# A delta-rule layer: the norms of queries and keys taken from transposed rows

## The reference, cut to what matters

```
def l2_norm(x):
    xf = x.astype(jnp.float32)
    return (xf * lax.rsqrt(jnp.sum(xf * xf, -1, keepdims=True) + EPS)).astype(x.dtype)

def deltanet_layer(x, valid, g_norm, w_in, conv_w, a_log, dt_bias, o_gain, w_out):
    ...
    z = h @ w_in
    qkv = jax.nn.silu(causal_dwconv(z[..., :2 * DN_KW + DN_VW], conv_w))
    ...
    q = l2_norm(q) * (DN_DK ** -0.5)
    k = l2_norm(k)
    ...
    o = gated_delta_rule(to_chunks(q), to_chunks(k), to_chunks(v), gate_chunks(g), gate_chunks(beta))
```

## Time and profile before

| what | value |
|---|---|
| median of 3 runs | 3075.04 us (3074.96 to 3075.6) |
| the profiled execution | 3068.84 us, of it the span 3066.8 us |
| TensorE busy | 2964.0 us, 97% of the span |
| VectorE busy | 1479.1 us, 48% |
| ScalarE busy | 798.5 us, 26% |
| GpSimd busy | 445.3 us, 15% |
| one-column products of the third layer | 160 records, 2191.8 to 2591.7 us |

### The profile page before, as it was taken

One profiled execution on the slowest core, in us unless ns is written; L12 is line 12 of the kernel. 1 busy time (PEld: TensorE's weight loads), 2 busy tenths in 40 slices (PEclk: granted clock), 3 DMA queues, 4 the chain that ended last, 5 costly groups with the idle time before them and its releaser, 6 DMA issues. The chain is left out here.

```text
span 3066.8 us, 38998 instructions
## 1 busy us (share of the span) xinstructions
PE 2964.0 (97%) x15091; PEld 1870.0 (61%) x15091; DVE 1479.1 (48%) x3453; ACT 798.5 (26%) x2045; POOL 445.3 (15%) x745
## 2 busy tenths in 40 slices
PE   5999999999999999799999999998999999999999
PEld 2445555555555554588787887654788888544444
DVE  2344544645545443555655665433445555443441
ACT  1113333323333321212323233221222222121230
POOL 0221221322212000121101112000001111111100
PEclk8999999999999999899999999999999999999999
DMA  7330001000113200421121211502421111030101
GB/s 248 130 145 28 28 28 54 30 28 28 35 49 90 76 1 21 148 62 53 45 76 46 66 49 51 176 1 83 110 56 29 29 41 44 1 114 26 55 1 55
DMA packets 137439, 186.78 MB, mean 61 GB/s; under 512 B 22284, under 2 KB 90540, under 8 KB 135204
## 3 DMA queue, kind: packets, MB, share of 16 engines
q1 hardware_dynamic: 136056, 184.21, 19.0%
q10 hardware_dynamic: 1200, 0.09, 0.0%
HBM read 174.61 MB, written 9.67 MB: 60 GB/s over the span
## 5 line engine op out<-in xcount | busy, mean ns | idle before, releaser
L488 PE MATMUL a_psP<-a_w,a_uT 128*128 128x512 f32 x1536 | 700.3, 601 | 7.5 <-DMA a_w<-a_w_in 7.5
L488 PEld LDWEIGHTS a_psP<-a_w,a_uT 128*128 128x128 f32 x1536 | 280.6, 192 | 325.0 <-issue 325.0
L737 DVE TENSOR_REDUCE a_small<-a_psS 128x1 f32<-128x768 f32 (+1 forms) x192 | 140.8, 775 | 402.0 <-PE a_psS L516 402.0
L1460 PE MATMUL b_psP<-b_w,b_uT 128*128 128x256 f32 x768 | 183.8, 382 | 1.0 <-DVE b_raw L1743 0.5
L643 ACT ACTIVATE a_e<-a_psS,a_small 128x768 f32<-128x768 f32 (+1 forms) x192 | 143.8, 753 | 139.1 <-DVE a_small L737 138.7
L1460 PEld LDWEIGHTS b_psP<-b_w,b_uT 128*128 128x128 f32 x768 | 141.7, 190 | 23.9 <-issue 3.9
L1780 DVE TENSOR_REDUCE b_small<-b_psS 128x2 f32<-128x512 f32 x64 | 44.3, 692 | 213.2 <-PE b_psS L1517 213.2
L650 ACT COPY a_pT<-a_psS 128x768 f32<-128x768 f32 (+1 forms) x96 | 63.0, 656 | 311.4 <-PE a_psS L525 311.4
L538 PEld LDWEIGHTS a_psO<-a_v,a_pT 128*128 128x128 f32 x896 | 115.1, 192 | 45.9 <-issue 45.9
L1617 ACT ACTIVATE b_e<-b_psS,b_small 128x512 f32<-128x512 f32 x128 | 86.7, 682 | 192.0 <-DVE b_small L1793 190.1
L1624 ACT COPY b_e<-b_psS 128x512 f32<-128x512 f32 x128 | 71.8, 587 | 228.6 <-PE b_psS L1527 147.4
(11 more groups left out here) (487 smaller groups left out, 5106.1 us busy)
## 6 DMA issues: line engine op xcount, KB each, us to landing
a_w<-a_w_in SPq DMA_DIRECT2D x16, 2048.0 KB, 9.0
b_w<-b_w_in SPq DMA_DIRECT2D x48, 512.0 KB, 3.8
a_yT<-mod_w SPq DMA_DIRECT2D x8, 1536.0 KB, 8.5
a_yT<-mod_w SPq DMA_DIRECT2D x8, 1024.0 KB, 17.5
b_yT<-b_w_in SPq DMA_DIRECT2D x16, 512.0 KB, 3.8
f_place<-bias_table SPq DMA_DIRECT2D x64, 128.0 KB
f_place<-a_w_in SPq DMA_DIRECT2D x16, 512.0 KB, 6.2
d_w<-a_w_in SPq DMA_DIRECT2D x16, 512.0 KB, 7.1
```

Source lines behind the costliest of these rows:

```text
L488: ins = nc.tensor.matmul(s.psP[:, x % 2, :], s.uT[:, a, t * P:(t + 1) * P], w[:, a, :], start=(a == 0), stop=(a == KD - 1))
L737: nc.vector.tensor_reduce(self.nm[i % 2][:, k:k + 1], self.score_banks(k, keys), AX_X, ALU.max, negate=True).then_inc(self.mx, 1)
L1460: ins = nc.tensor.matmul(out, lhsT, rhs, start=(a == 0), stop=(a == 3))
```

## The change

The squares are no longer summed by TensorE. Instead TensorE transposes the raw keys in step 0 (`key_rows`) and the raw queries in step 3 (`query_rows`) through `token_rows` into banks 5 and 6, so that tokens lie on partitions; ScalarE squares them out of these banks into `s.sq` (two ACTIVATEs each, 16 and 128 partitions); and VectorE adds up each token's 128 squares (`row_sums`: two reductions and the sum with epsilon). GpSimd's power is taken over five columns twice instead of ten once. The factors of the queries get a piece of their own in step 7 of VectorE's queue (`query_factors`).

The order changes with it. `log_decays` waits for ScalarE's squares of the keys. The pieces of `fold` in steps 3 and 4 (`BEHIND`) now come behind the projection products of their step, so `query_rows` stands behind the projections of step 3 and `query_products` behind those of step 4. On ScalarE the squares of the keys stand ahead of `tanh` in step 0, those of the queries at step 3 ahead of `copy_piece`, and the two squares of steps 9 and 10 are gone. On VectorE `query_sums` stands in step 5 ahead of two convolution passes.

```
@@ -1972,7 +1972,7 @@
         self.cv = sb("d_cv", [P, 2, TOK], F32)
-        self.sq = sb("d_sq", [P, 2, TOK], F32)
+        self.sq = sb("d_sq", [P, 2, CH * P], F32)
@@ -2233,7 +2233,7 @@
         chain.mark(nc.vector.tensor_scalar(row(EG), row(EG), 0.5, None, ALU.mult))
-        chain.mark(nc.vector.memset(s.ps[:, 6, 0:2 * CH], 0.0))
+        chain.mark(nc.vector.memset(s.tiny[:, 80:90], 0.0))
@@ -2264,6 +2264,7 @@
     PIECE = {1: 0, 3: 1, 4: 2, 5: 3, 7: 4, 9: 5, 10: 6, 11: 7}
+    BEHIND = (3, 4)
@@ -2274,11 +2275,13 @@
         (self.z, self.zc, self.cn, self.ct, self.si, self.gt, self.gz) = (sem("dh_" + n) for n in names)
-        names = ("squares", "square_sums", "sums_eps", "rstd", "factors", "log_decays", "decays", "kk",
+        names = ("key_squares", "key_rows", "sums_eps", "rstd", "factors", "log_decays", "decays", "kk",
                  "system", "kq", "attention", "keys_T", "keys_scaled", "values_T", "values_scaled", "first_level",
-                 "first_inverse_T", "first_inverse", "first_copied", "halves")
-        (self.sq, self.sm, self.se, self.rs, self.fa, self.gr, self.dm, self.kk, self.lt, self.kq, self.at,
-         self.tk, self.kd, self.tv, self.vb, self.b1, self.x1, self.x1T, self.x1c, self.hv) = (sem("df_" + n) for n in names)
+                 "first_inverse_T", "first_inverse", "first_copied", "halves", "query_rows", "query_squares",
+                 "query_sums_eps", "query_rstd", "query_factors", "row_sums")
+        (self.ks, self.kr, self.se, self.rs, self.fa, self.gr, self.dm, self.kk, self.lt, self.kq, self.at,
+         self.tk, self.kd, self.tv, self.vb, self.b1, self.x1, self.x1T, self.x1c, self.hv, self.qm, self.qs, self.qe,
+         self.qr, self.qf, self.rw) = (sem("df_" + n) for n in names)
@@ -2367,22 +2370,22 @@
-        def sums(h):
+        def key_rows(h):
                 self.prepare.gates_done(pe)
-            pe.wait_ge(self.sq, 2 * h + 2)
+            pe.wait_ge(self.si, 3 * h + 2)
                 pe.wait_ge(self.u0s, h - 1)
-            for r in range(2):
-                for t in range(CH):
-                    ins = nc.tensor.matmul(ps[0:chunk_len(t), 6, r * CH + t:r * CH + t + 1], s.sq[:, r, chunk_cols(t)],
-                                           s.masks[:, LEVELS + 1, 0:1], start=True, stop=True)
-            ins.then_inc(self.sm, 1)
+            token_rows(s.ck[:, h % 2, :], self.kr)
+
+        def query_rows(h):
+            pe.wait_ge(self.lt, h + 1)
+            token_rows(s.cq[:, h % 4, :], self.qm)
         def log_decays(h):
-            pe.wait_ge(self.se, h + 1)
+            pe.wait_ge(self.ks, h + 1)
@@ -2399,7 +2402,7 @@
         def query_products(h):
-            pe.wait_ge(self.lt, h + 1)
+            pe.wait_ge(self.qs, h + 1)
@@ -2432,7 +2435,7 @@
-        fold = {0: sums, 1: log_decays, 2: key_products, 4: query_products, 6: keys_T, 8: values_T, 10: first_inverse}
+        fold = {0: key_rows, 1: log_decays, 2: key_products, 3: query_rows, 4: query_products, 6: keys_T, 8: values_T, 10: first_inverse}
@@ -2581,7 +2584,7 @@
                             begin_rest(j)
-                if hf is not None and g in fold:
+                if hf is not None and g in fold and g not in self.BEHIND:
@@ -2589,6 +2592,8 @@
                         self.prepare.gate_sums(pe)
+                if hf is not None and g in self.BEHIND:
+                    fold[g](hf)
@@ -2622,12 +2627,12 @@
-        def squares(h, r):
-            act.wait_ge(self.si, 3 * h + r + 1)
+        def squares(h, r, rows, read, done):
+            act.wait_ge(rows, h + 1)
             if h:
-                act.wait_ge(self.sm, h)
-            x = s.cq[:, h % 4, :] if r == 0 else s.ck[:, h % 2, :]
-            nc.scalar.activation(s.sq[:, r, :], x, ACT.Square, scale=0.5).then_inc(self.sq, 1)
+                act.wait_ge(read, h)
+            nc.scalar.activation(s.sq[0:N_META, r, 0:P], ps[0:N_META, 6, P:2 * P], ACT.Square, scale=0.5)
+            nc.scalar.activation(s.sq[:, r, P:], ps[:, 5, :], ACT.Square, scale=0.5).then_inc(done, 1)
@@ -2689,7 +2694,10 @@
                     if g == 0:
+                        squares(hf, 1, self.kr, self.se, self.ks)
                         tanh(hf, 2)
+                    if g == 3:
+                        squares(hf, 0, self.qm, self.qe, self.qs)
@@ -2705,8 +2713,6 @@
                         tanh(hp, (6, 8).index(g))
-                    if g in (9, 10):
-                        squares(hp, g - 9)
@@ -2717,11 +2723,16 @@
         def rstd(h):
-            rs = s.tiny[:, 10:20]
             if h:
-                pool.wait_ge(self.fa, 5 * h)
-            nc.gpsimd.tensor_tensor(rs, s.tiny[:, 0:10], s.half[:, :], ALU.pow).then_inc(self.rs, 1)
+                pool.wait_ge(self.fa, 3 * h)
+            nc.gpsimd.tensor_tensor(s.tiny[:, 15:20], s.tiny[:, 5:10], s.half[:, 0:CH], ALU.pow).then_inc(self.rs, 1)
+
+        def query_rstd(h):
+            pool.wait_ge(self.qe, h + 1)
+            if h:
+                pool.wait_ge(self.qf, 2 * h)
+            nc.gpsimd.tensor_tensor(s.tiny[:, 10:15], s.tiny[:, 0:5], s.half[:, 0:CH], ALU.pow).then_inc(self.qr, 1)
@@ -2742,6 +2753,8 @@
                     rstd(hf)
+                if hf is not None and g == 5:
+                    query_rstd(hf)
@@ -2786,16 +2799,35 @@
+        def row_sums(h, r, chain):
+            raw = s.tiny[:, 80 + r * CH:80 + (r + 1) * CH]
+            nc.vector.reduce_sum(raw[0:N_META, 0:1], s.sq[0:N_META, r, 0:P], AX_X).then_inc(self.rw, 1)
+            nc.vector.reduce_sum(raw[:, 1:], by_chunk(s.sq[:, r, P:]), AX_X).then_inc(self.rw, 1)
+            dve.wait_ge(self.rw, 4 * h + 4 - 2 * r)
+            nc.vector.tensor_scalar(s.tiny[:, r * CH:(r + 1) * CH], raw, EPS, None, ALU.add).then_inc(chain, 1)
+
         def sums(h):
-            dve.wait_ge(self.sm, h + 1)
+            dve.wait_ge(self.ks, h + 1)
                 dve.wait_ge(self.rs, h)
-                dve.wait_ge(self.fa, 5 * h)
-            nc.vector.tensor_scalar(s.tiny[:, 0:10], ps[:, 6, 0:10], EPS, None, ALU.add).then_inc(self.se, 1)
+                dve.wait_ge(self.fa, 3 * h)
+            row_sums(h, 1, self.se)
+
+        def query_sums(h):
+            dve.wait_ge(self.qs, h + 1)
+            if h:
+                dve.wait_ge(self.qr, h)
+            row_sums(h, 0, self.qe)
+
+        def query_factors(h):
+            f, rq = s.fac[:, h % 4, :, :], s.tiny[:, 10:15]
+            dve.wait_ge(self.qr, h + 1)
+            nc.vector.tensor_scalar(f[:, FQ_ROW, :], rq, P ** -0.5, None, ALU.mult).then_inc(self.qf, 1)
+            nc.vector.tensor_scalar(f[:, FS_ROW, :], rq, 1.0 / P, None, ALU.mult).then_inc(self.qf, 1)
             f = s.fac[:, h % 4, :, :]
-            rq, rk, k2 = s.tiny[:, 10:15], s.tiny[:, 15:20], s.tiny[:, 5:10]
+            rk, k2 = s.tiny[:, 15:20], s.tiny[:, 5:10]
@@ -2803,9 +2835,7 @@
             nc.vector.scalar_tensor_tensor(f[:, NK_ROW, :], k2, 0.5, rk, ALU.mult, ALU.mult).then_inc(self.fa, 1)
-            nc.vector.tensor_scalar(f[:, FQ_ROW, :], rq, P ** -0.5, None, ALU.mult).then_inc(self.fa, 1)
-            nc.vector.tensor_scalar(f[:, FS_ROW, :], rq, 1.0 / P, None, ALU.mult).then_inc(self.fa, 1)
-            dve.wait_ge(self.fa, 5 * h + 1)
+            dve.wait_ge(self.fa, 3 * h + 1)
@@ -2817,7 +2847,7 @@
             dve.wait_ge(self.kk, h + 1)
-            dve.wait_ge(self.fa, 5 * h + 5)
+            dve.wait_ge(self.fa, 3 * h + 3)
@@ -2976,8 +3006,8 @@
                         silu(hf, 2)
-                    for at, f in ((1, factors), (2, system), (4, attention), (6, keys),
-                                  (8, values), (8, first_level), (8, first_inverse)):
+                    for at, f in ((1, factors), (2, system), (4, attention), (5, query_sums), (6, keys),
+                                  (7, query_factors), (8, values), (8, first_level), (8, first_inverse)):
```

## The result

The changed kernel takes 3044.19 us (median of 4 executions, 3043.09 to 3046.62) against 3075.0 us before on the same chip: a ratio of 0.9901, with a 95% interval of 0.9884 to 0.9919. In a second session it was 3047.98 us (5 executions, 3043.43 to 3052.68) against 3074.66 us: 0.9916 [0.9901, 0.9931]. The forecast was 3051.2 us with a range from 3046 to 3063: the direction and most of the size are right.

What follows compares the result with a forecast made beforehand. TensorE was taken to bound the kernel in the turns of heads 0 to 6. Savings of 2.1 + 16.6 + 2.7 + 2.4 = 23.8 us, off the median 3075.04 us, gave 3051.2 us, range 3046 to 3063.

Steps and rivals of the forecast that it cites:

- TensorE's products: Each head: one-column products out (2.16 us), two sets of five transposes in (1.10 us), net 1.06 us less at full clock.
- the sum: Third layer, all heads: savings of 2.1 + 16.6 + 2.7 + 2.4 = 23.8 us.
- The clock in heads 2 to 6: TensorE's clock no longer falls there: 4.14 us less for each of heads 2 to 5, 2.7 us for head 6.
- the stretch without a projection: TensorE's small products ahead of step 0's projections: shrinks from 4.05 to 2.03 us, so the clock stays up.
- the row of the fourth layer: Profile row at that layer's start: TensorE busy at 0.50 with transposes alone, 2730.06 to 2733.00; from 2733.40 at 1.00.
- The other queues: ScalarE, VectorE and GpSimd work stays covered at no cost; tightest VectorE's query side, slack 1.2 and 1.1 us.
- Head 7 and after: Head 7's turn, without projections: 0.9 + 2.7 - 1.25 = 2.4 us less; bounds 3.6 less and 0.3 more.
- the term of 1.25 us for VectorE's added work: Head 7's turn: query sums, 1.1 us, and factors, 0.15 us, in VectorE's chain taken off the saving.
- VectorE late: Rival: VectorE exceeds its 1.1 us slack, each microsecond beyond costing 7 us; with 1 us, 3058.2 us; chance 0.10.
- The clock that keeps falling: Rival: clock still falls despite the transposes, leaving only the products' difference, 7.1 us, 3067.9 us; chance 0.10.
- the rule behind it: Trainium skill, TensorE clock gate: transposes don't count as activity like other products and don't bring the clock up.
- The slower case: Rival: query-chain waits idle TensorE every turn and keep the clock down; 2.5 us a turn gives 3085 us; chance 0.03.

Runs made afterwards that it cites:

- the split: Kernel before with its ten one-column products divided, the keys' five moved behind the projections of step 0, no work removed: 3066.91 us, ratio 0.9970 to the kernel before.
- experiments 3 and 6: Changed kernel with keys transposed seven times in step 0: 3075.47 us; changed kernel with twenty one-column records put back before the key rows: 3079.79 us.
- experiment 4: Changed kernel with four more 128x512 reductions on VectorE in the query sums of step 5 each turn: 3056.05 us.
- experiment 1: Kernel before, unchanged, in 12 more executions: median 3075.16 us, ratio 1.0002; two further profiled executions took 3075.07 and 3077.77 us.

## Why the gain was larger than forecast

**TensorE's products: right.** Five transposes take 0.55 us, twice a head; the net 1.06 us a head at full clock is seen pure where the clock is up in both kernels: head 0 went from 38.76 to 37.61 us (1.15), head 1 from 53.56 to 52.62 (0.94), 2.1 us together as in the sum.

**The clock in heads 2 to 6: the size right for this pair of profiles, the reason half right.** The turns of heads 2 to 4 gave 4.24, 4.22 and 4.23 us (4.14 forecast), that of head 5 2.51, as the changed kernel has its fall there, that of head 6 2.83 (2.7). That the clock and not something else makes 3.1 us a turn is shown by the split (58.3 against 61.4 us with the same instructions), that one-column products bring it down and transposes don't by the pair of experiments 3 and 6. The prediction had two reasons. The first, that the stretch without a projection becomes shorter than the 2.92 and 2.68 us that left the clock up, does not hold: the same 2.92 us lost the clock in two other executions of the kernel before, 2.56 us lost it in two turns of the split, and 5.3 us of mostly transposes kept it. That this reason led to the right size is luck. The second, that transposes don't act like the one-column products (the row of the fourth layer), is the one that the runs bear out.

**The other queues: right.** Both sums, the later attention and the ScalarE copies cost TensorE nothing in heads 0 to 6, with a slack of 1.3 us at step 6 and 1.6 us at step 8. A third place, which the prediction did not name, is as tight as these: the transposes of `d_o` at step 7, 1.5 us (experiment 4). The lengths, forecast and measured: squares 0.98 and 0.27 + 0.57 us (0.17 + 0.57 back to back), reductions and sum 1.1 and 0.97 us, GpSimd's five columns up to 1.96 and 1.18 us for the keys, 1.62 for the queries.

**Head 7 and after: too small.** Against 2.4 us forecast, the end from head 7's key rows to the fourth layer gave 3.9 us (138.92 to 135.00), more than its upper bound of 3.6. What failed is the term of 1.25 us for VectorE's added work ("Against it VectorE gets the query sums in its chain"): the waits of TensorE in this turn are 4.0 us in both profiles, with 1.6 us for `d_XTc` before as after, so the added work costs nothing there. The line of before, which the prediction does not show:

```profile
PE d_ps L2456 <- DVE d_XTc L2883: 1.6, 3, 1.1
```

Without this term the sum is 3.6 us; the remaining 0.3 us has no cause shown.

**The step that failed**, beside that term, is in the clock and in the sum. The prediction put it as "In head 1 that stretch is 2.92 us (from 2229.82) and the clock stays" and then took the profiled execution for the median's: "the difference is taken off that". It was one execution, shorter than all 56 others. In two of three further ones the clock falls in heads 0 and 1 as well, 1.4 to 1.7 us each, which the change takes away. Over four profiles of each kernel, the difference by part is:

| part of the third layer | before, mean us | after, mean us | less |
|---|---|---|---|
| to the step-0 products of head 0 | 37.3 | 36.8 | 0.5 |
| heads 0 and 1 | 93.9 | 90.2 | 3.7 |
| heads 2 to 6 | 304.7 | 287.5 | 17.2 |
| head 7 to the fourth layer | 141.3 | 136.0 | 5.3 |
| sum | 577.2 | 550.6 | 26.6 |

So the like terms of the sum, 2.1, 19.3 and 2.4, should have been 3.7, 17.2 and 5.3: heads 0 and 1 and the end undersized, since the falls before were more frequent than in the one profile, heads 2 to 6 oversized, since the changed kernel has falls of its own behind the first inverse (2.68 us of 16 and 64 rows, which I took to leave the clock up; it does in 16 of 20 turns), and since the falls before cost less than 3.1 us in one of the profiles (59.7 to 60.0 us a turn, experiment 1). Four profiles of each kernel are few for such means: one end of 145.9 us makes 1.5 us of the 5.3. The mean spans of the same profiles, 3072.2 and 3045.6 us, differ by 26.6 too, so on the average nothing outside the layer takes part. The medians of 56 and 11 executions differ by 28.8; the last 2 us are within the spread of single executions, 13 us before and 10 after, and stay open, as does why the clock falls in heads 0 and 1 in some executions and not in others.

**The range.** It was too narrow for what it had to hold. The bounds that the prediction names give 3048.5 to 3058.0 us (1.2 and 1.5 us down, 2.7, 2.6 and 1.5 up), not its 3047 to 3056, and hardly any of this stands for falls of the clock that come and go between executions, though the median of the three runs was 6.2 us above the profiled execution. Of the chances, 0.74 + 0.10 + 0.05 is the 0.89 for faster; the rest adds up to 0.08 for same and 0.03 for slower, where 0.07 and 0.04 are written.

**The rivals.** VectorE late: not so, and experiment 4 shows what it costs where it is, 0.9 us a turn. The clock that keeps falling: not in step 0, where no turn of heads 0 to 6 in the four profiles after has a fall, and the rule behind it does not hold here. The slower case needed 3.6 us in VectorE's queue; there was none.

## What to carry to other kernels

Products with one column cost more than their own time when many stand together: they can bring TensorE's clock down for the projections behind them, here mostly 1.4 to 3.1 us a turn beside 2.2 us of products. Look at the granted clock over a turn and not only at busy shares, and try an order with the narrow products apart before taking work out (8 to 10 of the 29 us here). One profile tells one execution: where the clock falls in some turns and not in others, take several profiles, or a range wide enough for the falls that this one happened not to have.

## What the runs showed of the hardware

The clock can fall after 2.2 us of one-column products (head 0 of the kernel before in experiment 1, 0.72) and stay up through 3.85 us of nothing but transposes (1.00). The same instructions in the same order lose it in one turn and not in the next (58.3 and 64.4 us). A reduction over 128x512 out of SBUF takes 0.67 us, a square of 128x512 out of PSUM 0.57 us, GpSimd's power of five columns 1.18 us, and that same instruction at another place of the turn 1.62 us, both in the turn of head 3 of the changed kernel.
